# Moving operands of the matmuls placed at other addresses modulo 512: a two-block transformer kernel on one core

## The chip, the cores and the metric

The kernel runs on one core of one Trainium2 chip. The metric is the device time of one execution in microseconds, lower is better. Before the change it is 2701.14 us, the median of 3 runs (2697.59 to 2708.88).

## What is computed

One token sequence of 256 tokens and width 2048 goes through two transformer blocks, all in float32.

```python
x  = first_block(x, c, ctx, ...)
#   h = modulate(rms_norm(x), ...); split_projection(h @ w_in)        w_in   [2048, 3904]
#   latent attention + short convolution, x += gate * merge_heads(...) @ w_out
#   x += gate * ((a * silu(g)) @ w_down),  a, g = dwconv3(h @ w_up)   w_up [2048, 11008], w_down [5504, 2048]
out = second_block(x, ...)
#   z = rms_norm_2(x) @ w_in_2; two attentions, a @ w_proj_a, b @ w_proj_b, merged @ w_out_2
#   x += square(relu(rms_norm_2(x) @ w_up_2)) @ w_down_2              w_up_2 [2048, 8192], w_down_2 [8192, 2048]
```

Activations are held transposed: features on the 128 partitions, the 256 tokens along the free axis. The time goes to the large products with weights that are read once.

## The kernel before

**Split weights.** Each float32 product is made of three passes over values rounded to fp32r. The SyncE queue loads weights in chunks of 2 k-tiles x 512 columns (512 KB) into a ring of 8 slots, `raw` (`load`, L419 in the profile). ScalarE copies a chunk into one of 4 slots of `whi` (`split`, L618), VectorE writes the remainder raw - whi into the same slot of `wlo` (L1100). ScalarE's copy waits until TensorE has used the chunk that lay in the slot four chunks before.

**The matmuls.** `product` runs over the chunks, their k-tiles and the four blocks of 128 output features. `block` issues three matmuls for each: whi with the high half of the activations (L1887), whi with their low half (L1888), wlo with the high half (L1889). The weights are the standing operand (128x128, a row of 512 bytes in each partition), the activations the moving one (256 tokens, 1024 bytes). Each matmul has its own weight load (PEld in the profile). A tile of activations `x[:, k, :]` has 512 elements: 256 high, 256 low. So a product with 16 k-tiles is 16 x 4 x 3 = 192 matmuls.

**Other uses of the same tiles.** `token_product` makes h2 the standing operand and moves whi and wlo, 512 columns each (L1921 to L1923). `key_values` does the same with `kvn` for the values of block one, 256 columns in two runs of 128 (L2076 to L2078), and then the products on `h` or `mix` go on. `add_folded` puts the sums of squares between the chunks of some products (L2192), `mod` (L1858) and `attend` the matmuls of the modulation and of attention.

**The order** is written out by hand in one program for each engine. TensorE: modulation; w_in, attention and w_out of block one (to some 590 us); FFN of block one on hf, hid0 (twice) and hid1; from 1323 us on block two: w_in_2 on h2 with attention, gates and projections on h2 and heads2, w_out_2 on merged; and then the FFN of block two, which goes from hf to hid0 or hid1 and back every four groups of 192 matmuls.

**Where the operands lie.** SBUF tensors are placed one behind another in the order of the `sb(...)` calls, each rounded up to 32 bytes, on top of a reserved scratch of 16,384 bytes and 128 bytes of constants. In one partition, in bytes:

| tile | address | modulo 512 | operand |
|---|---|---|---|
| whi, wlo | 65,664 and 82,048 | 128 | weights |
| h1, hctx, mix, qn, kvn | 149,312 to 206,656 | 320 | moving, block one before the FFN |
| hf, h2 | 130,880 | 320 | moving |
| hid0, heads2_0 | 163,648 | 320 | moving |
| heads2_1 | 180,032 | 320 | moving |
| hid1, merged | 196,416 | 320 | moving |

Rows of weights are 512 bytes apart and tiles of activations 2048, with the low half at +1024, so each operand keeps its residue modulo 512 throughout. The last byte used is 229,184 of 229,376. In the profile the buffer numbers are left out (hid is hid0 or hid1, h is h1 or h2, heads is heads2).

The matmuls of a block:

```python
def block(o, b, hi, lo, x, k, nk):
    mm(o, hi, x[:, 0:T], start=(k == 0 and b % 2 == 0), stop=False, skip_group_check=True)
    mm(o, hi, x[:, T:2 * T], start=False, stop=False, skip_group_check=True)
    return mm(o, lo, x[:, 0:T], start=False, stop=(k == nk - 1), skip_group_check=True)
```

Of the kernel before, what the change touches and what calls it, by code (L numbers as in the profile page):

```python
# [8 lines left out]
P = 128  # L9
D = 2048  # L10
T = 256
# [14 lines left out]
HT = 16  # L26
# [8 lines left out]
F32R = mybir.dt.float32r  # L35
# [153 lines left out]
def program(nc, ins, consts, out, known, traced):  # L189
    with ExitStack() as ctx:  # L190
        def sb(name, shape, dt=F32, scope=ctx):
            return scope.enter_context(nc.sbuf_tensor(name, shape, dt))
# [109 lines left out]
        sc = ExitStack()  # L302
# [10 lines left out]
        sc = ExitStack()  # L313
# [19 lines left out]


        sc = ExitStack()
        hf = sb("hf", [P, KT, 2 * T], F32R, scope=sc)
        hid = [sb(f"hid{i}", [P, HT, 2 * T], F32R, scope=sc) for i in range(2)]
        sc.close()


        sc = ExitStack()
        h2 = sb("h2", [P, KT, 2 * T], F32R, scope=sc)
        heads2 = [sb(f"heads2_{i}", [P, HEADS, 2 * T], F32R, scope=sc) for i in range(2)]
        sc2 = ExitStack()
        q2 = sb("q2", [P, 2, 4, T], scope=sc2)
        k2 = sb("k2", [P, 2, 4, T], scope=sc2)
# [11 lines left out]
        sc = ExitStack()  # L358
# [2065 lines left out]
```

## Time and profile before

| | |
|---|---|
| median of 3 runs | 2701.14 us |
| the profiled execution's own span | 2701.8 us |
| TensorE busy | 2606.8 us, 96% |
| VectorE, ScalarE, GpSimd busy | 65%, 45%, 4% |
| matmuls | 21,322 |
| read from HBM | 548.53 MB, 204 GB/s over the span |
| mean granted clock of TensorE | 0.984 of full speed |

Times in the profile count from the start of the span. PE is TensorE's matmuls, PEld its weight loads, DVE VectorE, ACT ScalarE, POOL GpSimd, SP SyncE. A matmul is drawn from its start to its modelled end, so the records of successive matmuls overlap; the distance between starts is what TensorE needs for one. A window of the profile lists for each engine the time that it was busy and, in brackets, the instructions that touch the window; behind them stand the granted clock (1.00 is 2.4 GHz), the share of the DMA engines and GB/s.

### The profile page before, as it was taken

The page shows a single profiled execution, that of the slowest core. Times are in us where ns is not written, and L with a number is a line of the kernel's source. Part 1 is how long each engine was busy: PE and PEld are TensorE (multiplying, and loading weights), DVE is VectorE, ACT ScalarE, POOL GpSimd, SP SyncE. Part 2 cuts the span into 40 slices and gives each one's busy share as a digit, 9 for nine tenths or more (in the row PEclk, how much of TensorE's full clock was granted, in tenths as well). Part 3 has the DMA queues.
Part 4 walks back from the last instruction along what each step waited for, and adds up shares of the span by engine and source line. Part 5 has one row for each costly group of instructions (what it writes and reads, how often), then busy time and mean ns, then how long its engine had stood idle before and what let it go on. Part 6 is the DMA issues. An engine that isn't in the chain of part 4 may idle for free.

```text
span 2701.8 us, 51009 instructions
## 1 busy us (share of the span) xinstructions
PE 2606.8 (96%) x21322; PEld 2522.5 (93%) x21322; DVE 1758.9 (65%) x2033; ACT 1222.5 (45%) x1487; POOL 112.5 (4%) x196
## 2 busy tenths in 40 slices
PE   6899988989999999999999999999999999999998
PEld 4699877889999999999999999999999999999997
DVE  5989776778888755665865655555665555555554
ACT  6753333345454544444544445444444444434433
POOL 0000323300000000000000110000000000000000
PEclk9899999989999999999999999999999999999999
DMA  9878766757777665565665555666566666666662
GB/s 353 283 227 271 254 210 206 240 174 242 250 242 250 208 198 173 168 220 175 197 189 155 180 159 160 194 194 193 192 183 195 193 195 194 189 194 195 194 210 95
DMA packets 289063, 553.55 MB, mean 205 GB/s; under 512 B 19386, under 2 KB 28712, under 8 KB 288232
## 3 DMA queue, kind: packets, MB, share of 16 engines
q1 hardware_dynamic: 288328, 548.53, 63.8%
q8 instruction: 141, 2.31, 0.3%
q10 hardware_dynamic: 544, 2.29, 0.2%
q14 instruction: 50, 0.41, 0.0%
HBM read 548.53 MB, written 2.10 MB: 204 GB/s over the span
## 4 chain that ended last, share of the span: by engine, by line
PE 84%; DVE 9%; ACT 3%; issue 2%; DMA 1%; POOL 1%; SPq 0%; ACTq 0%; DVEq 0%; POOLq 0%
PE half L1887 25%; PE half L1889 25%; PE half L1888 25%; DVE wlo L1100 4%; DMA raw<-in_w_ada 1%; ACT whi L618 1%; DVE acc L1129 1%; PE half L1921 1%; PE half L1923 1%; PE half L1922 1%; DVE acc L1132 1%; DVE tmp L1213 0%; PE half L2168 0%; PE half L2141 0%; PE half L2140 0%
## 5 line engine op out<-in xcount | busy, mean ns | idle before, releaser
L1100 DVE TENSOR_TENSOR wlo<-raw,whi 128x1024 fp32r<-128x1024 f32 (+1 forms) x909 | 1089.3, 1211 | 777.5 <-ACT whi L618 775.7
L618 ACT ACTIVATE whi<-raw 128x1024 fp32r<-128x1024 f32 (+1 forms) x909 | 940.5, 1048 | 1038.6 <-PE half L1889 922.6
L1887 PE MATMUL half<-hf,whi 128*128 128x256 f32 x2400 | 668.2, 278 | 6.4 <-DVE hf L1192 5.2
L1888 PE MATMUL half<-hf,whi 128*128 128x256 f32 x2400 | 666.2, 278 | 0.0
L1889 PE MATMUL half<-hf,wlo 128*128 128x256 f32 x2400 | 666.2, 278 | 0.0
L1887 PE MATMUL half<-hid,whi 128*128 128x256 f32 x1712 | 475.0, 277 | 1.2 <-DVE wlo L1100 1.2
L1888 PE MATMUL half<-hid,whi 128*128 128x256 f32 x1712 | 474.4, 277 | 0.0
L1889 PE MATMUL half<-hid,wlo 128*128 128x256 f32 x1712 | 474.4, 277 | 0.0
L1887 PEld LDWEIGHTS half<-hf,whi 128*128 128x128 f32 x2400 | 451.3, 188 | 8.5 <-issue 5.8
L1889 PEld LDWEIGHTS half<-hf,wlo 128*128 128x128 f32 x2400 | 453.0, 189 | 0.0
L1888 PEld LDWEIGHTS half<-hf,whi 128*128 128x128 f32 x2400 | 452.1, 188 | 0.0
L1887 PE MATMUL half<-h,whi 128*128 128x256 f32 x1520 | 428.9, 282 | 5.6 <-issue 3.8
L1888 PE MATMUL half<-h,whi 128*128 128x256 f32 x1520 | 423.2, 278 | 0.0
L1889 PE MATMUL half<-h,wlo 128*128 128x256 f32 x1520 | 423.0, 278 | 0.0
L1887 PEld LDWEIGHTS half<-hid,whi 128*128 128x128 f32 x1712 | 321.6, 188 | 2.2 <-issue 1.7
L1889 PEld LDWEIGHTS half<-hid,wlo 128*128 128x128 f32 x1712 | 322.5, 188 | 0.0
L1888 PEld LDWEIGHTS half<-hid,whi 128*128 128x128 f32 x1712 | 321.5, 188 | 0.0
L1887 PEld LDWEIGHTS half<-h,whi 128*128 128x128 f32 x1520 | 286.8, 189 | 8.2 <-issue 5.7
L1888 PEld LDWEIGHTS half<-h,whi 128*128 128x128 f32 x1520 | 287.0, 189 | 0.6 <-issue 0.2
L1889 PEld LDWEIGHTS half<-h,wlo 128*128 128x128 f32 x1520 | 287.5, 189 | 0.0
L1132 DVE SCALAR_TENSOR_TENSOR acc<-raw,silu_sb,acc 128x512 f32<-128x512 f32 x128 | 96.2, 752 | 4.5
L1129 DVE SCALAR_TENSOR_TENSOR acc<-raw,silu_sb,acc 128x512 f32<-128x512 f32 x112 | 84.4, 753 | 12.0 <-DVE wlo L1100 0.5
(290 smaller groups left out, 3020.4 us busy)
## 6 DMA issues: line engine op xcount, KB each, us to landing
raw<-in_w_up SPq DMA_DIRECT2D x288, 512.0 KB, 4.3
raw<-in_w_in SPq DMA_DIRECT2D x216, 512.0 KB, 4.0
raw<-in_w_down SPq DMA_DIRECT2D x212, 512.0 KB, 4.5
raw<-in_w_ada SPq DMA_DIRECT2D x192, 512.0 KB, 5.2
raw<-in_w_out SPq DMA_DIRECT2D x64, 512.0 KB, 4.8
raw<-in_w_proj_a SPq DMA_DIRECT2D x16, 512.0 KB, 4.5
raw<-in_w_proj_b SPq DMA_DIRECT2D x16, 512.0 KB, 4.2
raw<-in_w_up SPq DMA_DIRECT2D x16, 384.0 KB, 3.4
```

What stands on the lines that cost most here:

```text
L618: A(whi[:, s, 0:elems], raw[:, c, 0:elems], ACT.Copy).then_inc(s_hi_ready, 1)
L1100: V.tensor_tensor(wlo[:, s, 0:elems], raw[:, c, 0:elems], whi[:, s, 0:elems].bitcast(F32), ALU.subtract).then_inc(s_drained, 1)
L1129: V.scalar_tensor_tensor(a, w[:, 0, :], s[:, 0:1], a, ALU.mult, ALU.add).then_inc(s_dve_step, 1)
L1132: V.scalar_tensor_tensor(a, w[:, 1, :], s[:, 1:2], a, ALU.mult, ALU.add).then_inc(s_drained, 1)
L1887: mm(o, hi, x[:, 0:T], start=(k == 0 and b % 2 == 0), stop=False, skip_group_check=True)
L1888: mm(o, hi, x[:, T:2 * T], start=False, stop=False, skip_group_check=True)
L1889: return mm(o, lo, x[:, 0:T], start=False, stop=(k == nk - 1), skip_group_check=True)
L1921: mm(o, xh, hi, start=(k == 0), stop=False)
L1922: mm(o, xh, lo, start=False, stop=False)
L1923: ins_ = mm(o, xl, hi, start=False, stop=(k == nk - 1))
```

## The change

```diff
         sc = ExitStack()
+        sb("below_hf", [P, 32], scope=sc)
         hf = sb("hf", [P, KT, 2 * T], F32R, scope=sc)
-        hid = [sb(f"hid{i}", [P, HT, 2 * T], F32R, scope=sc) for i in range(2)]
+        sb("below_hid0", [P, 64], scope=sc)
+        hid0 = sb("hid0", [P, HT, 2 * T], F32R, scope=sc)
+        sb("below_hid1", [P, 96], scope=sc)
+        hid = [hid0, sb("hid1", [P, HT, 2 * T], F32R, scope=sc)]
         sc.close()
 
 
         sc = ExitStack()
+        sb("below_h2", [P, 32], scope=sc)
         h2 = sb("h2", [P, KT, 2 * T], F32R, scope=sc)
+        sb("below_heads2", [P, 64], scope=sc)
         heads2 = [sb(f"heads2_{i}", [P, HEADS, 2 * T], F32R, scope=sc) for i in range(2)]
+        sb("below_merged", [P, 96], scope=sc)
         sc2 = ExitStack()
...
-        nc = bacc.Bacc("TRN2", target_bir_lowering=False, num_devices=1)
+        nc = bacc.Bacc("TRN2", target_bir_lowering=False, num_devices=1, dynamic_dma_scratch_size=8192)
```

The margins have 32, 64 and 96 elements of 4 bytes: 128, 256 and 384 bytes. They put hf and h2 at 448, hid0 and heads2 at 192, and hid1 and merged at 64 bytes modulo 512. The scratch for DMA descriptors at the bottom of SBUF shrinks from 16,384 to 8,192 bytes, which makes room for the margins, and all tensors move down by 8,192 bytes. whi and wlo stay at 128 modulo 512, and the moving operands of block one before its FFN at 320. The tensors that share the place of merged (q2, k2, v2, the masks, sig_b) move with it.

## Rows read from the trace of the kernel before

**Rows 1.** The page: TensorE in the span, and the chain that ended last.

```profile
PE 2606.8 (96%) x21322; PEld 2522.5 (93%) x21322; DVE 1758.9 (65%) x2033; ACT 1222.5 (45%) x1487; POOL 112.5 (4%) x196
...
PE 84%; DVE 9%; ACT 3%; issue 2%; DMA 1%; POOL 1%; SPq 0%; ACTq 0%; DVEq 0%; POOLq 0%
```

**Rows 2.** Busy time of each engine in three parts of the program.

```profile
590.00:1323.00 733.00, 725.38 (x6238) 721.88 (x6236) 523.28 (x641) 353.19 (x417) 0.00 (x0) 0.99 0.63 207
1323.00:2688.00 1365.00, 1362.94 (x11454) 1341.52 (x11452) 780.27 (x784) 600.19 (x670) 19.58 (x16) 1.00 0.60 183
```

**Rows 3.** Windows in the 24 long-spacing stretches: length, busy (matmuls), clock, DMA.

```profile
922.70:1145.50 222.80, 222.80 (x1894) 1.00 0.58 180
...
1956.70:1978.90 22.20, 22.20 (x191) 1.00 0.59 180
...
sum 507.70, PE 507.70; mean PE 21.15
```

**Rows 4.** The same for the 36 stretches at the shorter spacing.

```profile
1677.80:1932.80 255.00, 255.00 (x2252) 1.00 0.62 192
2003.30:2633.40 630.10, 630.10 (x5562) 1.00 0.64 195
...
sum 1392.70, PE 1392.70; mean PE 38.69
```

**Rows 5.** One-column matmuls of the modulation, in order of time (start, us).

```profile
697.50 0.28 PE L1889 MATMUL half<-hf,wlo 128*128 128x256 f32 x1
697.63 1.05 PE L1858 MATMUL half<-ones,acc 128*128 128x1 f32 x8
```

**Rows 6.** Value matmuls of pair 0 and the product after, by time.

```profile
222.66 0.28 PE L2076 MATMUL half<-whi,kvn 128*128 128x256 f32 x1
...
225.27 0.28 PE L2078 MATMUL half<-whi,kvn 128*128 128x256 f32 x1
225.39 0.28 PE L1887 MATMUL half<-h,whi 128*128 128x256 f32 x1
...
228.10 0.28 PE L1889 MATMUL half<-h,wlo 128*128 128x256 f32 x1
```

**Rows 7.** Value matmuls of pair 3, in order of time.

```profile
434.29 0.28 PE L2076 MATMUL half<-whi,kvn 128*128 128x256 f32 x1
...
437.00 0.28 PE L2078 MATMUL half<-whi,kvn 128*128 128x256 f32 x1
```

**Rows 8.** Starts after the square sums (L2192), in order of time.

```profile
1932.96 0.59 PE L2192 MATMUL half<-tmp,ones 128*128 128x256 f32 x2
1933.20 0.47 PE L1887 MATMUL half<-merged,whi 128*128 128x256 f32 x1
...
2002.09 0.60 PE L2192 MATMUL half<-tmp,ones 128*128 128x256 f32 x2
2002.34 0.47 PE L1887 MATMUL half<-hf,whi 128*128 128x256 f32 x1
```

**Rows 9.** The instructions on tile hf.

```profile
L1887 PE MATMUL half<-hf,whi x2400: 276/276/551, 596.6 to 2508.1; 128*128 128x256 f32 x185
...
L958 ACT ACTIVATE hf<-xt,vec x16: 493/496/512, 1920.4 to 1990.1; 128x256 fp32r<-128x256 f32 x16
```

**Rows 10.** The split, 2003 to 2633 us: busy, mean ns, idle before, releaser.

```profile
L618 ACT ACTIVATE whi<-raw 128x1024 fp32r<-128x1024 f32 x232 | 246.3, 1062 | 353.5 <-PE half L1889 353.5
```

**Rows 11.** DMA queues of the page.

```profile
q1 hardware_dynamic: 288328, 548.53, 63.8%
...
q10 hardware_dynamic: 544, 2.29, 0.2%
```

## The prediction

> **What bounds the kernel now.** I began with the page. TensorE is busy for 96% of the span and holds 84% of the chain that ended last [rows 1]. The three parts of the program tell where: behind 590 us, in the FFN of block one and in all of block two, TensorE is idle for 733.00 - 725.38 = 7.6 us and 1365.00 - 1362.94 = 2.1 us [rows 2]. What the change moves lies behind 590 us, so there the time is the number of matmuls times the distance between their starts, and every other engine is cover.
>
> A busy TensorE says nothing of that distance, because a matmul is drawn 0.28 us long [rows 9] while the next starts 0.11 us later. So I counted starts in stretches without a break. A window counts matmuls in flight at its left edge too, so the distance is (window + 0.28) / count. Two values come out and hardly anything between. From 922.70 to 1145.50 us it is 223.08 / 1894 = 117.8 ns [rows 3]; from 2003.30 to 2633.40 us it is 630.38 / 5562 = 113.3 ns [rows 4]. The form is the same (128x128 weights, 256 columns), the granted clock is 1.00 in both (2.4 GHz), and so are the addresses modulo 512: moving operand at 320, weights at 128. So the address alone does not choose between the two. Behind 590 us 24 stretches with 507.7 us in them go at 117.8 [rows 3], and 36 with 1392.7 us at 113.3 [rows 4]. A stretch keeps its value until something other than these products comes between. That something can be small: the same L2192 matmuls come before the product at 1933.20, which stays at 117.8, and before the one at 2002.34, which is at 113.3 within 1 us and stays there for 630 us [rows 3, 4, 8].
>
> **The change, part by part.** It removes and adds no instruction, transfer or wait. It does three things to addresses.
>
> (1) The DMA scratch shrinks from 16,384 to 8,192 bytes, and everything above it moves down by 8,192. That is 16 x 512, so no residue changes. The scratch would serve transfers whose descriptors software writes; all loads go through hardware queues [rows 11]. Cost 0. If some hidden use of it existed, it would show as a longer time to landing, and the split would cover it: ScalarE's copy waits for TensorE to free a slot for 353.5 us over 232 copies there, 1.52 us each [rows 10].
>
> (2) The margins cost space alone: no instruction touches them. The engines that write the moved tiles do so beside the matmuls, as the 16 roundings into hf at 496 ns [rows 9]. If one of them became longer by some ns, the idle engines of rows 2 would hide it (ScalarE 600 of 1365 us busy). Cost 0.
>
> (3) The moving operand's place relative to the weights. Before, it is 320 - 128 = 192 bytes everywhere. After: hf and h2 448 - 128 = 320; hid0 and heads2 192 - 128 = 64; hid1 and merged 64 - 128 = 448 (mod 512). This touches 7,200 matmuls on hf, 5,136 on hid, 3,072 on h2 (as moving operand), 768 on heads2 and 768 on merged, together 16,944; 1 ns on each is 16.9 us. It is the only term with a price, and no row prices it for 64 or 448. One row prices 320. In key_values the value matmuls have the weights moving (128) and kvn standing (320), so moving minus standing is -192 = 320 mod 512. In pair 0, 24 of them go from 222.66 to 225.27 us, 2.61 / 23 = 113.5 ns [rows 6]; in pair 3 from 434.29 to 437.00, 2.71 / 23 = 117.8 ns [rows 7]. So at 320 I see the same two values as at 192. Its moving pattern is two runs of 128 columns, which is the weakness of the comparison. The bounds for each residue are therefore the two levels. All stretches at 113.3: 507.7 x (1 - 113.3 / 117.8) = 19.4 us less. All at 117.8: 1392.7 x (117.8 / 113.3 - 1) = 55.3 us more. Below 113.3 I find no support: eight one-column matmuls, whose moving operand can't hold anything up, stand (1.05 - 0.25) / 7 = 0.114 us apart (0.25 us being such a matmul's own length, my estimate from the 0.28 of a wide one) [rows 5], so the weight load sets this pace. I take 0, the value of the nearest row (kvn's), and keep both ends.
>
> The Trainium skill has a rule that would leave more to win: "TensorE: Matmul & The Clock Gate", section "Back-to-back issue gap", gives 262 cycles for 256 columns when warm, which is 109.2 ns. No stretch here is at it; if the new places reached it, my estimate from that page is 2701.8 - 507.7 x (1 - 109.2 / 117.8) - 1392.7 x (1 - 109.2 / 113.3) = 2614 us.
>
> The sum is 0 + 0 + 0 against a span of 2701.8 us. The median of the three runs is 2701.14, 0.7 us under it, and the lowest 2697.59. I forecast 2700 us: between those two, since a shift of a few short stretches is worth 1 us or so each (a stretch of 191 matmuls is 191 x 4.5 ns = 0.9 us) and may go either way. An effect under 0.5%, 13.5 us, is what a measurement of this kernel can't tell from no change.
>
> **Rivals.**
> *Slower, by the long stretches.* The 630 us stretch and the 255 us stretch owe their 113.3 ns to one start each. Until now the addresses are alike when the product goes from hf to hid and back, and the value survives. After the change each such step alters the relation (320, 64, 320, 448). Where the relation alters today without a gap, the distance has grown: kvn's value matmuls at 113.5 ns are followed at 225.39 us by 24 on h that take 2.71 / 23 = 117.8 ns [rows 6]. If this catches the stretch at 2003.30 it costs 630.1 x (117.8 / 113.3 - 1) = 25.0 us, 2727 us in all; with the stretch at 1677.80, 255.0 x 0.0397 = 10.1 us more, 2737 us; all of them give 2757 us. It decides from 13.5 / 0.0397 = 340 us of stretch that change from 113.3 to 117.8. Against it: that step also goes from weights that move to weights that stand, which no step from hf to hid does.
> *Faster: the places do away with 117.8.* If the longer distance is a meeting of the two reads that only some distances between the addresses allow, the new ones may have none. Then all 24 stretches fall to 113.3, and the time is 2701.8 - 19.4 = 2682 us. For it: the longer distance keeps over 1,894 matmuls, so it has a cause that repeats with each matmul, as addresses do. Against: kvn's 117.8 at 320 [rows 7].
> *Faster beyond that,* at the page's 109.2 ns or near it: about 2614 us, nothing in the trace for it.
> *The change does nothing.* The sizes are multiples of 32 bytes, so each margin shifts by just its own bytes: 320 + 128 = 448; 448 + 256 = 704, 192; 192 + 384 = 576, 64. If the residues came out otherwise, 2701 us.
>
> **How the numbers follow.** No measurable effect 0.36, and 0.02 that the residues are not what the change says: same 0.38, at 2700 us. Slower by the long stretches 0.32. Faster at 113.3 everywhere 0.28 and beyond it 0.02: faster 0.30. The forecast's own range is 2690 to 2713. The whole range goes down to 2676, the 2682 of the faster rival less 6 for the spread of the runs (2697.59 to 2708.88) and for a little more won in the first part; and up to 2737, both long stretches lost. What it leaves out is the loss of nearly all stretches and the gain beyond 113.3, below 2 in 10.
>
> **What would show it.** Right, if the windows behind 590 us again give 117.8 and 113.3 ns and nothing new, with some 500 us of stretches at the former. Wrong, if a tile has one level in all its stretches (hf, hid0 or hid1), if a third value appears, if the value changes at the step from hf to hid near 2160 us, or if the time comes from before 590 us, where all residues stay. The instructions of ScalarE and VectorE on hf and hid should keep their durations, and the number of instructions should be the same.

## The result and the profile after

The changed kernel takes 2745.25 us (median of 4 runs, 2741.71 to 2751.99), the kernel before 2704.9 us beside it (4 runs, 2697.59 to 2708.88). The ratio is 1.0148, with a 95% interval of 1.0128 to 1.0168: 40 us slower. The forecast was 2700 us with a range up to 2737. A trace shows one execution of a kernel; that of the changed kernel took 2751.99 us, the longest of its four, so the two spans lie further apart (48.4 us) than the medians.

The page of the changed kernel, TensorE in the span and the chain that ended last:

```profile
PE 2658.9 (97%) x21322; PEld 2574.8 (94%) x21322; DVE 1761.3 (64%) x2033; ACT 1224.2 (45%) x1487; POOL 114.8 (4%) x196
...
PE 85%; DVE 8%; ACT 2%; issue 2%; DMA 1%; POOL 1%; SPq 0%; ACTq 0%; DVEq 0%; POOLq 0%
```

The same 21,322 matmuls keep TensorE busy for 52.1 us more than in [rows 1], in a span 48.4 us longer (2750.2 against 2701.8). VectorE and ScalarE are within 2.4 us of what they were. So the work is the same and only TensorE's pace has changed. The parts of the changed kernel, in the columns of [rows 2] (the number of matmuls stands in the first brackets):

```profile
590.00:1323.00 733.00, 726.17 (x6115) 724.17 (x6116) 512.88 (x626) 347.01 (x404) 0.00 (x0) 0.99 0.63 203
1323.00:2688.00 1365.00, 1364.66 (x11179) 1341.39 (x11178) 767.13 (x774) 592.28 (x659) 19.63 (x16) 1.00 0.60 183
```

TensorE idles as little as before (6.8 and 0.3 us), but gets through 6,115 matmuls where [rows 2] had 6,238, and 11,179 where it had 11,454. Windows inside the 48 stretches at the longer spacing, in the form of [rows 3]:

```profile
1697.60:1923.50 225.90, 225.90 (x1921) 1.00 0.60 187
...
2031.40:2376.00 344.60, 344.60 (x2928) 1.00 0.62 186
2463.20:2644.00 180.80, 180.80 (x1537) 1.00 0.62 192
...
sum 1779.10, PE 1779.10; mean PE 37.06
```

and inside the 5 stretches at the shorter spacing, in the form of [rows 4]:

```profile
1923.70:1961.40 37.70, 37.70 (x335) 1.00 0.56 180
2376.20:2463.00 86.80, 86.80 (x768) 1.00 0.62 193
...
sum 189.90, PE 189.90; mean PE 37.98
```

Counted as in the prediction, the two values are unchanged: (344.60 + 0.28) / 2928 = 117.8 ns, (86.80 + 0.28) / 768 = 113.4 ns. What changed is how much stands at each. Before, 1392.7 us of stretches, 73%, went at 113.3 ns [rows 3, 4]; now 189.9 us, 10%. That is 1392.7 / 0.1133 - 189.9 / 0.1133 = 10,600 matmuls that cost 4.5 ns more, some 47.7 us, beside a growth of the span by 48.4 us. Of that growth 2.5 us lie ahead of the first matmul on hf (at 599.1 us, before at 596.6), where no residue changed; it starts between 592.7 and 601.1 us in the kernels below, so I take it for the spread of executions.

The two steps in the chain of block two's FFN, in order of time. First from hf (at 448) to hid1 (at 64), then from hid1 back to hf:

```profile
2374.80 0.28 PE L1896 MATMUL half<-hf,wlo 128*128 128x256 f32 x1
...
2375.97 0.28 PE L1894 MATMUL half<-hid,whi 128*128 128x256 f32 x1
...
2376.21 0.28 PE L1896 MATMUL half<-hid,wlo 128*128 128x256 f32 x1
...
2377.11 0.28 PE L1895 MATMUL half<-hid,whi 128*128 128x256 f32 x1
```

```profile
2462.23 0.28 PE L1896 MATMUL half<-hid,wlo 128*128 128x256 f32 x1
...
2463.02 0.28 PE L1894 MATMUL half<-hf,whi 128*128 128x256 f32 x1
...
2463.61 0.28 PE L1896 MATMUL half<-hf,wlo 128*128 128x256 f32 x1
```

Ten distances on hf take 1.17 us (117 ns), eight on hid1 0.90 us (113 ns). Going back, seven take 0.79 us (113 ns), and then five on hf 0.59 us (118 ns). No pause lies between; the operand alone changes. The kernel before never does this at such a step.

### The profile page after: what moved, and what is told of

Read it like the earlier page. It is cut to its first block, busy times and chain, and to the rows that moved or that the text cites. A ratio compares the mean times of both kernels' runs of the same rounds, so it can differ in the third digit from the quotient of the medians.

```text
span 2750.2 us, 51009 instructions
## 1 busy us (share of the span) xinstructions
PE 2658.9 (97%) x21322; PEld 2574.8 (94%) x21322; DVE 1761.3 (64%) x2033; ACT 1224.2 (45%) x1487; POOL 114.8 (4%) x196
## 4 chain that ended last, share of the span: by engine, by line
PE 85%; DVE 8%; ACT 2%; issue 2%; DMA 1%; POOL 1%; SPq 0%; ACTq 0%; DVEq 0%; POOLq 0%
PE half L1894 26%; PE half L1895 26%; PE half L1896 25%; DVE wlo L1107 3%; DMA raw<-in_w_ada 1%; DVE acc L1136 1%; ACT whi L625 1%; PE half L1928 1%; PE half L1930 1%; PE half L1929 1%; DVE acc L1139 1%; PE half L2017 1%; PE half L2018 0%; DVE tmp L1220 0%; PE half L2275 0%
```

## The experiments

I call the address of the moving operand minus that of the weights, modulo 256 or 512, the distance, as the texts on record do, and the time from one matmul's start to the next the pace: 113.3 or 117.8 ns. Before, every product has distance 192. After, hf and h2 have 320, hid0 and heads2 64, hid1 and merged 448. Modulo 256 that is 64, 64 and 192. A distance of 192 modulo 256 I call good, any other bad. "Share" below is the part of the stretches behind 590 us that goes at 113.3 ns, in the one execution that was traced.

### Which of the parts costs

The first kernel keeps the smaller scratch and drops all margins; the others keep one margin's effect each (a second margin puts what lies above back to 320):

```diff
-        sb("below_hf", [P, 32], scope=sc)
-        sb("below_hid0", [P, 64], scope=sc)
-        sb("below_hid1", [P, 96], scope=sc)
...
```

These lines are against the changed kernel; the three margins of block two go in the same way. That is e1_scratch. e2_hf has 32 elements below hf and 96 below hid0, e3_hid0 96 below hid0 and 32 below hid1, e4_hid1 64 below hid1, and each the same below h2, heads2 and merged.

> The scratch is halved, all margins are gone: moving operands at 320 again, everything 8,192 bytes lower. Theory A (the distance from the weights' address to the moving operand's, modulo 256 or 512, decides whether matmuls can go 113.3 ns apart) and theory B (each step between operands at different distances throws the sequence back to 117.8 ns): within 5 us of the kernel before, about 2702 us, hf at 113 ns in three matmuls of four. Theory C (the smaller scratch or the 8 KB shift costs the time): about 2745 us.

> hf and h2 alone at 448, hid, heads2 and merged at 320. Theory A: all matmuls that move hf or h2 stand 117.8 ns apart; by tile, after minus before, that is 21.8 us on hf, 8.5 on h2 and 1.6 on the token products that hold h2, 32 us in all, about 2735 us, and up to 13 us more where hid0 and hid1 take over the 117.8 ns from hf. Theory B gives the same in the FFN of block two, but leaves the stretches inside hf and h2 as they start, so about 2720 us.

> hid0 and heads2 alone at 192, all others at 320. Theory A: hid0 and heads2 wholly at 117.8 ns, 8.3 + 3.4 = 12 us more, and what follows them without a break (two groups of hf and two of hid1 behind hid0 in block two, h2 behind heads2) up to 20 us more: 2713 to 2733 us. Theory B: the same, so this run only shows whether hf can come back to 113 ns behind hid0.

> hid1 and merged alone at 64, 448 from the weights. Theory A: at 448 both distances are possible as at 192, so no change within 5 us, about 2702 us, and hid1 keeps 113.3 ns in block two. Theory B: the step from hf to hid1 throws block two's FFN to 117.8 ns, from the first hid1 group in it to the last matmul, so at least 13 us more, 2714 us or above.

| kernel | moved | us | ratio to before, 95% interval | share |
|---|---|---|---|---|
| e1_scratch | nothing, scratch halved | 2711.2 | 1.0020 (1.0003 to 1.0037) | 58% |
| e2_hf | hf, h2 to 448 | 2732.1 | 1.0096 (1.0079 to 1.0113) | 28% |
| e3_hid0 | hid0, heads2 to 192 | 2744.2 | 1.0143 (1.0126 to 1.0160) | 26% |
| e4_hid1 | hid1, merged to 64 | 2707.1 | 1.0004 (0.9986 to 1.0021) | 61% |

The scratch and the shift by 8 KB cost at most 0.4%; theory C (the scratch or the shift) is out. Moving hid1 and merged costs nothing, and theory B, that any step between different distances throws the sequence back, falls with it: the long stretch after 2,008 us of e4_hid1 contains steps between 192 and 448 and stays at (630.00 + 0.28) / 5561 = 113.3 ns.

```profile
2008.00:2638.00 630.00, 630.00 (x5561) 1.00 0.64 195
```

With hf and h2 alone at 448 the tiles alternate by themselves. Windows of e2_hf: heads2 (320), h2 (448), hid0 (320), hf (448), and then, by itself, one on hid1 and hid0 (320) in the FFN of block one:

```profile
1687.50:1708.00 20.50, 20.50 (x183) 1.00 0.61 186
1709.00:1753.00 44.00, 44.00 (x376) 1.00 0.58 185
2182.00:2267.00 85.00, 85.00 (x753) 1.00 0.64 193
2269.00:2358.00 89.00, 89.00 (x758) 1.00 0.63 186
```

```profile
1175.00:1290.00 115.00, 115.00 (x979) 1.00 0.55 176
```

113.6, 117.8, 113.2 and 117.8 ns: in these two chains each entry onto the bad distance goes to 117.8 at once, each entry onto the good one back to 113.3. The last window shows that the second is no rule: there hf at 448 goes before, and the tiles at 320 stay at 117.8 ns (115.28 / 979). Every operand at 448 stands at 117.8, as theory A has it, but for some 60 matmuls on h2. The 26 us over the kernel before are less than its 32 us. In the trace hf starts 3.9 us earlier than in the kernel before (592.7 against 596.6), which is part of the difference.

e3_hid0 was missed: expected 2713 to 2733 us, measured 2744 (the traced execution took 2734.5, the shortest of four). Its two bad tiles are small (3,600 matmuls), but in the last chain the good ones are at 117.8 as well. hf and hid0 from 2,010 us on, and hf again:

```profile
2010.50:2172.00 161.50, 161.50 (x1374) 1.00 0.64 186
2173.50:2262.00 88.50, 88.50 (x754) 1.00 0.61 186
2264.00:2353.00 89.00, 89.00 (x758) 1.00 0.62 186
```

All stand at 117.8 ns (89.28 / 758). hf at distance 192 can hold either value; here it has the long one from its start near 2,009 us on, and 5,500 matmuls keep it.

### Other distances

> Three new distances in one kernel: hf and h2 at 128 (distance 0 from the weights), hid0 and heads2 at 160 (32), hid1 and merged at 224 (96). Theory A says that each of them has a fixed character, to be read in all stretches of its tile: either only 117.8 ns, as at 64 and 320, or both values, as at 192 and 448; with a rule modulo 256 in which 192 is the good one, the neighbours 32 and 96 of the bad 64 would be bad too, distance 0 open. Theory B (steps between distances cost): 117.8 ns nearly throughout behind 1323 us whatever the tile.

> The next three: hf and h2 at 256 (distance 128), hid0 and heads2 at 288 (160), hid1 and merged at 352 (224). Theory A with 192 as the middle of the good distances: 160 and 224 show 113.3 ns as well, 128 open; if one of them shows 113.3 ns alone, with no stretch of over 50 matmuls at 117.8, it is the place for a faster kernel. Theory B: 117.8 ns nearly throughout, as in the run before it.

> The weights move to 256 modulo 512. hf and h2 lie at 320, where they lay in the kernel before, but now at distance 64; hid0, heads2 and the first part's tiles at 448, now at distance 192; hid1 and merged at 0, distance 256. Theory A (the distance counts): hf and h2 only at 117.8 ns, hid0 and heads2 show 113.3. Theory C (the moving operand's own address counts): the other way round, hf as in the kernel before with three in four at 113.3 ns, hid0 and heads2 wholly at 117.8 as hf was in the changed kernel.

The edit is the size of the margins, and in f3_weights one of 32 elements below whi. Windows of hf, hid0 and hid1 in f1_near (0, 32, 96), the same in f2_mid (128, 160, 224), and heads2, hf and hid1 in f3_weights (192, 64, 256):

```profile
2046.00:2210.00 164.00, 164.00 (x1369) 1.00 0.62 182
2213.00:2300.00 87.00, 87.00 (x741) 1.00 0.61 187
2396.00:2484.00 88.00, 88.00 (x736) 1.00 0.60 182
```

```profile
2037.00:2199.00 162.00, 162.00 (x1367) 1.00 0.63 184
2202.00:2289.00 87.00, 87.00 (x744) 1.00 0.62 186
2383.00:2470.00 87.00, 87.00 (x738) 1.00 0.60 187
```

```profile
1690.00:1710.00 20.00, 20.00 (x179) 1.00 0.61 186
2025.00:2186.00 161.00, 161.00 (x1370) 1.00 0.63 186
2370.00:2458.00 88.00, 88.00 (x736) 1.00 0.60 183
```

| distance modulo 256 | 0 | 32 | 64 | 96 | 128 | 160 | 192 | 224 |
|---|---|---|---|---|---|---|---|---|
| ns between starts | 120.0 | 117.8 | 117.7 | 119.9 | 118.7 | 117.3 | 113.3 | 118.3 |

Distance 256 gives 119.9 ns, as distance 0 gives 120.0. Each was executed once: f1_near 2780.64 us, f2_mid 2765.43, f3_weights 2752.93, beside 2706.0 for the kernel before. In these windows only 192 goes at 113.3. A place can have a second value, though: in f1_near the first stretch on heads2, at 32, goes at 116.6 ns (20.28 / 174), and in f2_mid hid0, at 160, goes at 118.6 from 965 us (85.28 / 719).

```profile
1706.00:1726.00 20.00, 20.00 (x174) 1.00 0.60 180
```

```profile
965.00:1050.00 85.00, 85.00 (x719) 1.00 0.59 185
```

The hope in the expectation of f2_mid, a place with 113.3 alone, is gone, and so is the idea that the neighbours of 192 are good too. f3_weights speaks against the moving operand's own address: at 320, where the kernel before has it at 113.3 for three matmuls in four, hf is at 117.7, and heads2 at 448, the place where the changed kernel has hf at 117.8, is at 113.3. One part of its expectation failed: hid0, at 192 as well, is at 117.8 in the chain from 2,023 us, 85.28 / 724.

```profile
2190.00:2275.00 85.00, 85.00 (x724) 1.00 0.62 186
```

### Distance or own address

h1_weights_too keeps the moving operands where the change put them; i2_all_bad leaves the FFNs' and block two's at 320, where they were. In both, the weights move to 256, by the line below. i1_all64 has one margin of 256 bytes for all. Theory C is, since f3_weights, that the moving operand's own address counts.

```diff
+        sb("below_whi", [P, 32])
         whi = sb("whi", [P, NSPLIT, CW], F32R)
```

> The changed kernel's moving operands stay just where the change put them (448, 192, 64), and only the weights move, from 128 to 256 modulo 512. Theory A (the distance modulo 256, 192 being the one place with 113.3 ns): hf, h2, hid0 and heads2 are at 192 again and get 113.3 ns back in most stretches; hid1 and merged are at 320 = 64 modulo 256 and stand at 117.8 throughout, 2,061 x 4.5 ns = 9.3 us and 336 x 4.5 ns = 1.5 us over the kernel before. Together about 2716 us, a ratio near 1.004. Theory C (the moving operand's own address): 2745 us as the changed kernel.

> One margin of 256 bytes in place of three: hf, h2, hid0, heads2, hid1 and merged all at 64, where the change put hid1 and merged, 448 from the weights (192 modulo 256). Theory A in its present form: at 192 modulo 256 both distances in time hold themselves, at 64 only the longer one; so every one of these tiles shows stretches at 113.3 ns again, and the time is near the kernel before, 2700 to 2712 us, or 25 us over that if the start near 2,010 us falls to 117.8. Theory C (an address of its own): hf and h2 unlike before, no statement. Theory D (moving an operand off 320 or having margins costs something by itself): near the changed kernel, 2745 us.

> No moving operand of the FFNs and of block two leaves 320, where the kernel before has them; the weights alone move, from 128 to 256 modulo 512, so that the distance is 64 for all of these 16,944 matmuls (the first part's tiles follow the weights and stay at 192). Theory A: 117.8 ns nearly throughout behind 590 us, 55 us over the kernel before, about 2757 us, ratio 1.018 to 1.021, slower than the changed kernel, whose hid1 and merged are at a good distance. Theory D and theory C (the moving operand's own address): as the kernel before, about 2705 us.

| kernel | weights | moving (hf and h2, hid0 and heads2, hid1 and merged) | distance modulo 256 | us | ratio, 95% interval | share |
|---|---|---|---|---|---|---|
| h1_weights_too | 256 | 448, 192, 64 | 192, 192, 64 | 2736.0 | 1.0087 (1.0055 to 1.0120) | 24% |
| i1_all64 | 128 | 64, 64, 64 | 192, 192, 192 | 2711.4 | 1.0014 (0.9999 to 1.0028) | 65% |
| i2_all_bad | 256 | 320, 320, 320 | 64, 64, 64 | 2751.9 | 1.0172 (1.0149 to 1.0195) | 12% |

i1_all64 and i2_all_bad came out as theory A has them: a margin as such costs nothing (theory D is out), and the moving operands' old addresses are as slow as the change's once the weights have moved away (1.0172 against 1.0148, with intervals that overlap, so the order of the two that was expected is not shown). The 2757 us were 5 us too many, since at distance 64 some stretches do hold 113.3. Of i2_all_bad the longest of its ten, and their sum:

```profile
1155.10:1287.80 132.70, 132.70 (x1174) 1.00 0.60 198
...
sum 227.00, PE 227.00; mean PE 22.70
```

So "only 117.8 at 64" was too strong: 113.3 can hold itself there, but is seldom reached.

h1_weights_too was a miss, 20 us over its expectation. heads2 is back at 113.3 and merged at 117.8 as foretold (first two rows), but the chain of hf and hid from 2,012 us stands at 117.8 though hf and hid0 have distance 192 (third row):

```profile
1685.00:1705.00 20.00, 20.00 (x179) 1.00 0.64 187
1903.00:1941.00 38.00, 38.00 (x325) 1.00 0.56 182
2012.00:2665.00 653.00, 653.00 (x5547) 1.00 0.62 188
```

Either weights at 256 were bad by themselves, or it was again the start near 2,010 us. The last four kernels shift weights and every moving operand together, so that each product keeps distance 192.

```diff
+        sb("below_whi", [P, 32])
         whi = sb("whi", [P, NSPLIT, CW], F32R)
```

The line is against e1_scratch. The width is 32 elements in j1_shift128, 16 in j2_shift64, 96 in j3_shift384 and 64 in j4_shift256.

> Weights at 256, every moving operand at 448: the kernel before shifted by 128 bytes, all distances 192. If the distance alone decides, the start near 2,010 us may fall either way, 2705 or 2730 us, and hf in the FFN of block one shows some stretches at 113.3 ns. If the weights' own residue counts (256 bad), hf and hid stand at 117.8 ns as in the run with the weights at 256 before it, 2735 us or more, h2 included.

> Weights at 192, moving operands at 384, distance 192. Distance alone: near 2705 us, or 2730 if the long start falls. Own residue: no statement for 192, but a third level or none at 113.3 would show it.

> Weights at 0, moving operands at 192, distance 192. Distance alone: near 2705 us, or 2730 if the long start falls. Own residue modulo 256: as the shift by 128, since 0 and 256 are the same modulo 256, so 2735 us or more if that one is.

> Weights at 384, moving operands at 64, distance 192; all addresses equal those of the kernel before modulo 256. If only addresses modulo 256 count, this is the kernel before to the stretch: 2705 us, the 630 us stretch at 113.3 ns included. If it falls to 2730 us, a start is a matter of more than these residues.

| kernel | weights, moving | us | ratio, 95% interval | share |
|---|---|---|---|---|
| j1_shift128 | 256, 448 | 2707.5 | 0.9999 (0.9983 to 1.0015) | 62% |
| j2_shift64 | 192, 384 | 2710.5 | 1.0007 (0.9995 to 1.0019) | 65% |
| j3_shift384 | 0, 192 | 2710.8 | 1.0011 (0.9997 to 1.0024) | 70% |
| j4_shift256 | 384, 64 | 2704.95 | 0.9989 (0.9976 to 1.0002) | 68% |

All four are the kernel before, within the measurement, and weights at 256 are no worse than others. At distance 192, with the weights at 0, 128, 192, 256 and 384, the own addresses don't count; the distance does. The long stretch of block two's FFN is at 113.3 ns in each, here j4_shift256, (624.00 + 0.28) / 5509:

```profile
2006.00:2630.00 624.00, 624.00 (x5509) 1.00 0.62 195
```

That settles h1_weights_too as far as the weights go: it was the start. In all the eight kernels in which every product has distance 192 modulo 256 (before, e1_scratch, e4_hid1, i1_all64 and these four), the chain of hf and hid from near 2,010 us is at 113.3 ns. Of the ten in which some product has another, the changed kernel and e2_hf have 113.3 in it wherever the distance is 192; e3_hid0, f3_weights, h1_weights_too and the two kernels below have 117.8 even there; and f1_near, f2_mid and i2_all_bad have no operand at 192 in it.

### A try at a kernel faster than both

Since stepping from a bad onto a good distance had mostly brought 113.3 ns, I gave the first tile of hf a bad distance, so that each product might start itself over.

```diff
-        hf = sb("hf", [P, KT, 2 * T], F32R, scope=sc)
+        sb("below_hf", [P, 32], scope=sc)
+        hf = Shifted(sb("hf", [P, KT * 2 * T + 32], F32R, scope=sc), (0,))
+        sb("below_hid0", [P, 64], scope=sc)
...
```

The lines are against the kernel before, with the smaller scratch. `Shifted` (left out here) hands out tile 0 at the start of the tensor and the tiles behind it 32 elements further up. Here tile 0 of hf stands at 448, and tiles 1 to 15 at 64; hid0 and hid1 stay at 320. g2_kick_both also does the same with h2, whose tiles 0, 4 and 10 stand at 448 and the others at 64.

> Only the first of the 16 tiles of hf lies at 448 (distance 320), the 15 others at 64 (distance 448), all else as before. In the runs so far a sequence at 117.8 ns on a bad distance that stepped without a pause onto a good one went to 113.3 within a few matmuls. If that holds for a step after 12 matmuls, every product on hf is at 113.3 ns from its second tile on: the 1,825 matmuls of hf at 117.8 become 37 x 12 = 450, 6 us less, and hid0 takes the value over in the FFN of block one, 3 us more: about 2696 us, ratio 0.996. If the long distance is a matter of how a product starts and nothing else, 450 matmuls more at 117.8: 2704 us, ratio 1.001.

> The same in hf, and in h2 the tiles 0, 4 and 10 at a bad distance, which are those that follow the pauses for attention. If a bad tile brings the sequence back to 113.3 ns, h2's 1,091 matmuls at 117.8 become 16 x 36 = 576, some 2 us less than the run before it, about 2694 us; if not, 3 us more than it.

Both are slower: 2732.3 us, ratio 1.0079 (1.0056 to 1.0103), and 2739.7 us, ratio 1.0108 (1.0083 to 1.0133). The chain of hf and hid from near 2,010 us, which starts in the middle of a product, on a good tile, is at 117.8 ns throughout, here from 2,011 us in g1_kick_hf, 653.28 / 5547:

```profile
2011.00:2664.00 653.00, 653.00 (x5547) 1.00 0.62 188
```

So the bad tiles don't bring it 113.3 ns. But a bad tile doesn't take 113.3 away either. In g2_kick_both the chain of heads2 and h2 from 1,686 us is at 113.3 ns from its start, and h2 has 18 bad tiles in it: at each the pace goes to some 118 ns and is back at 113.3 within a few matmuls behind it. The window of the first six of them holds 370 matmuls, 114.3 ns each; at 117.8 throughout it would hold 359.

```profile
1708.00:1750.00 42.00, 42.00 (x370) 1.00 0.60 190
```

The same can be read for whole tensors. In e3_hid0 the FFN of block one goes from hf (192) to hid0 (64) and back to hf, from 925 us: 113.4, 117.8 and 113.3 ns.

```profile
925.00:955.00 30.00, 30.00 (x267) 1.00 0.58 197
958.00:1043.00 85.00, 85.00 (x724) 1.00 0.60 187
1048.00:1142.00 94.00, 94.00 (x832) 1.00 0.58 173
```

The 18 traces have 18 such passages without a pause, from whole tensors at 192 over others and back to 192 (in the changed kernel, e2_hf, e3_hid0, f3_weights and h1_weights_too). In all 18 the pace after is the pace before, 11 times 113.3 and 7 times 117.8. The reading that fits them is that a bad distance hides the pace that a chain has, and the step back shows it again. No run tested this by itself, and a pace can change inside a chain: in the kernel before it goes from 117.8 to 113.3 at 676.4 us, within hf and without a pause, and in g1_kick_hf at 623.6 us, behind a bad tile. At distance 32 it doesn't hold (116.6 ns on heads2 before the first passage through h2 in f1_near, 117.8 after it).

Bad tiles that are one in sixteen of hf cost as much as hf wholly at a bad distance (1.0079 against 1.0096 in e2_hf), mostly because the 5,547 matmuls from 2,011 us on are all at 117.8 ns. No kernel of this study is measurably faster than the one before.

## Why the prediction was wrong

**What bounds the kernel** was right: the pace of the matmuls behind 590 us, at two levels, and nothing else. Parts (1) and (2) of the change cost nothing measurable, as forecast. e1_scratch is at 1.0020 with more of hf at 117.8, but j4_shift256, with the same small scratch, is at 0.9989, so this looks like the start of stretches and not the scratch. ScalarE's writes into the moved hf kept their length, 497 ns against 496 in [rows 9]:

```profile
L965 ACT ACTIVATE hf<-xt,vec x16: 494/497/511, 1949.0 to 2018.7; 128x256 fp32r<-128x256 f32 x16
```

**The step that failed is the value taken for part (3),** "I take 0, the value of the nearest row (kvn's)". The row showed 24 matmuls at 113.5 ns with the roles of the operands exchanged and a moving pattern of two runs [rows 6]. That said 113.3 is possible at such a distance, which the runs confirm (i2_all_bad has 1,174 in a row at 64). It did not say how often it is reached, and the cost lay there: the share fell from 73% to 10%, and the term came to some 47.7 us in place of 0. Nor could a row with the roles exchanged price the new places: the token products, which have them exchanged too, go faster at moving minus standing 64 modulo 256 than at 192, the reverse of the other products (last section). I had treated the residue as irrelevant because one address had both values. Both statements go together: at a good distance a chain has either value, mostly from its start on, and at 64 it has nearly always the longer one.

**The upper bound held.** "All at 117.8: 55.3 us more" encloses the measured 40 us, and the span's 48.4 us are 88% of it. The bound belonged in the range; I cut the range at the two longest stretches, 2737 us, and the median came out 8 us above. The reason is that the loss was given its chance (0.32) as a matter of luck for single stretches, where the distance acts on all of them alike. The 0.5% that I called the limit of such a measurement was too wide as well: the interval of the ratio is 0.2% to either side.

**The rival "slower, by the long stretches"** named the right price per matmul, the right place (the stretches at 1,698 and 2,031 us, now at 117.8 but for hid1 and merged) and the right sign. Its mechanism was wrong: not each change of distance breaks 113.3 (e4_hid1 has three in that stretch, all between 192 and 448, and loses nothing), and one onto a bad distance slows the matmuls there and not those that follow at a good one. Of the signs of being wrong that I named, two nearly came: a tile with one level in all its stretches (hf, hid0 and heads2 at 117.8, while hid1 and merged have both), and a change of value at a step from hf to hid (at 2,376 us, not near 2160).

**The rival "faster"** was right that the distance of the addresses counts, and had the sign wrong: the kernel before already sits at the one good place. That two reads meet is not shown by any run.

**The rule of the Trainium skill**, 109.2 ns for 256 columns ("TensorE: Matmul & The Clock Gate", "Back-to-back issue gap"), is given there for an isolated matmul, not for a stream in which each has its own weight load. This stream reached it at none of the eight distances; the lowest was 113.3.

**What stays open:** what decides the pace at a start, why the chain from near 2,010 us has 113.3 ns in all eight kernels with one distance and 117.8 in e3_hid0, h1_weights_too and the two kernels with a bad tile, which start it on a good distance too, what changes a pace inside a chain, and what in the chip depends on the distance. The traces show starts and not accesses, so no run here can tell.

## What to carry to other kernels

Count starts in a window: a TensorE that is 97% busy at full clock can still be 4% off its pace, and neither the busy share nor the length of a matmul shows it. Where 128x128 fp32r weights alternate with 256 moving columns, hold the distance between the two addresses at 192 modulo 256 for all products of a chain, and check it after each new tensor or margin: a single tile of hf off it lost 20 us here. A row in which something is possible at a new setting prices the best case, not the usual one.

## What the runs showed of the hardware that was not expected

The pace of weight load and matmul depends on the difference of their addresses modulo 256 bytes (119.9 ns at 256, 120.0 at 0), not on either alone, as far as 192 and 64 were tried at several addresses, with 113.3 ns at 192 and 116.6 to 120.0 at the seven other multiples of 32. At 192 two paces hold themselves, at 64 as well but rarely the short one, and a pace passes on from product to product over thousands of matmuls without a break, in most cases over a bad distance too.

The token products, 512 moving columns with h2 standing, depend on it in another way. From the second to the last start of the first of them, 94 steps:

```profile
1370.96 0.39 PE L1922 MATMUL half<-wlo,h 128*128 128x512 f32 x1
...
1392.47 0.39 PE L1923 MATMUL half<-whi,h 128*128 128x512 f32 x1
```

```profile
1386.35 0.39 PE L1929 MATMUL half<-wlo,h 128*128 128x512 f32 x1
...
1408.29 0.39 PE L1930 MATMUL half<-whi,h 128*128 128x512 f32 x1
```

```profile
1392.71 0.40 PE L1929 MATMUL half<-wlo,h 128*128 128x512 f32 x1
...
1414.06 0.39 PE L1930 MATMUL half<-whi,h 128*128 128x512 f32 x1
```

That is 228.8 ns in the kernel before (moving minus standing 64 modulo 256), 233.4 in the changed one (192) and 227.1 in f1_near (0). In each kernel the four token products agree within 1 ns, so this form shows one pace for each distance; the lowest is at 0, where the products with 256 columns have their highest, and 192 is the worst of these three. The distance to look for is one of the form of instruction.
